# Query and key pieces of the second layer as one 512-column product each, with the attention of a head pair between the pieces

## What is computed

```
h = rms_norm_2(x, g_pre_mix)
q, k, v = split_heads(h, w_qkv)             # 16 heads of 64, w_qkv is 1024 x 3072
for each chunk of 64 tokens c:              # 4 chunks, a query sees its chunk and all before it
    sc = q_blk @ k[:k1].T / 8 + bias
    o  = softmax(sc) @ v[:k1]
m = merge_heads(o) @ w_o
x = x + rms_norm_2(m, g_post_mix)
```

## Time and profile before

| What | Value |
|---|---|
| Median of 3 runs | 884.66 us (884.55 to 884.75) |
| The profiled execution | 885.27 us |
| Its span, first to last instruction | 883.4 us |
| PE busy | 872.6 us, 99% of the span, 4882 matmuls |
| DVE busy | 619.0 us, 70% |
| ACT busy | 441.2 us, 50% |
| Stage of the eight pieces, first product to first matmul after the last piece | 597.57 to 656.61 us |

### The profile page before, as it was taken

The page is one execution under the profiler, slowest core; times in us unless marked ns, Lnnn a source line. Parts: engine busy times, 40 slices in busy tenths (PEclk is TensorE's granted clock), DMA queues, the critical chain, the costliest instruction groups (busy, mean ns, idle before and its releaser), DMA issues.

```text
span 883.4 us, 12485 instructions
## 1 busy us (share of the span) xinstructions
PE 872.6 (99%) x4882; PEld 749.4 (85%) x4882; DVE 619.0 (70%) x785; ACT 441.2 (50%) x587; POOL 78.5 (9%) x114
## 2 busy tenths in 40 slices
PE   9999999999999999999999999999999999999996
PEld 8988888888888988788888888879987888888885
DVE  5999877766666678857666666775675676676674
ACT  4795454433333587745333333464565644434432
POOL 3663110000000020011000000010000200000000
PEclk9999999999999999999999999999999999999999
DMA  9754346565554371376655555547433456565541
GB/s 295 235 202 180 115 171 229 166 220 191 188 192 176 108 214 49 124 258 193 218 190 192 193 188 192 181 150 232 137 104 96 143 155 226 191 200 180 190 144 48
DMA packets 97818, 155.87 MB, mean 176 GB/s; under 512 B 4079, under 2 KB 72332, under 8 KB 97772
## 3 DMA queue, kind: packets, MB, share of 16 engines
q1 hardware_dynamic: 95068, 149.37, 50.4%
q0 software_dynamic: 1648, 5.80, 2.0%
q10 hardware_dynamic: 1056, 0.07, 0.1%
HBM read 153.62 MB, written 1.09 MB: 175 GB/s over the span
## 4 chain that ended last, share of the span: by engine, by line
PE 90%; DVE 4%; ACT 2%; issue 2%; POOL 0%; DVEq 0%; POOLq 0%; ACTq 0%
PE psum L2011 19%; PE psum L1917 17%; PE psum L1918 17%; PE psum L1919 16%; PE psum L2014 10%; PE psum L2456 2%; ACT w_hi L758 1%; DVE w_lo L1241 1%; PE psum L2486 1%; PE psum L2563 1%; PE psum L2469 1%; PE psum L1938 1%; PE psum L2239 1%; PE psum L2574 1%; PE psum L1976 1%
## 5 line engine op out<-in xcount | busy, mean ns | idle before, releaser
L1241 DVE TENSOR_TENSOR w_lo<-raw,w_hi 128x2048 fp32r<-128x2048 f32 (+3 forms) x116 | 260.2, 2251 | 90.7 <-ACT w_hi L758 47.5
L2011 PE MATMUL psum<-h_both,w_hi 128*128 128x512 f32 x800 | 199.4, 391 | 0.2 <-DVE w_lo L1241 0.2
L2011 PEld LDWEIGHTS psum<-h_both,w_hi 128*128 128x128 f32 x800 | 146.2, 188 | 28.1 <-DVE w_lo L1241 0.4
L758 ACT ACTIVATE w_hi<-raw 128x2048 fp32r<-128x2048 f32 (+2 forms) x71 | 129.5, 1837 | 36.5 <-PE psum L1919 35.0
L1917 PE MATMUL psum<-w_hi,g_hi 128*128 128x512 f32 x368 | 144.8, 394 | 0.9 <-DVE g_lo L1850 0.9
L1918 PE MATMUL psum<-w_lo,g_hi 128*128 128x512 f32 x368 | 143.7, 390 | 0.0
L1919 PE MATMUL psum<-w_hi,g_lo 128*128 128x512 f32 x368 | 143.3, 389 | 0.0
L776 ACT ACTIVATE w_hi<-raw 128x2048 fp32r<-128x2048 f32 x66 | 125.3, 1909 | 23.9 <-PE psum L1919 23.9
L2014 PEld LDWEIGHTS psum<-h_both,w_lo 128*128 128x128 f32 x800 | 109.1, 190 | 7.8
L2014 PE MATMUL psum<-h_both,w_lo 128*128 128x256 f32 x800 | 111.5, 282 | 0.0
L943 ACT ACTIVATE g_hi<-g_mul 128x512 fp32r<-128x512 f32 x32 | 20.3, 634 | 163.3 <-DVE g_mul L1556 163.3
(11 more groups left out here) (291 smaller groups left out, 1117.5 us busy)
## 6 DMA issues: line engine op xcount, KB each, us to landing
raw<-in_ffn_w SPq DMA_DIRECT2D x64, 1024.0 KB, 5.3
raw<-in_w_qkv SPq DMA_DIRECT2D x12, 1024.0 KB, 5.3
raw<-in_ab_w_in SPq DMA_DIRECT2D x11, 1024.0 KB, 5.7
raw<-in_w_gate SPq DMA_DIRECT2D x11, 1024.0 KB, 5.3
raw<-in_w_up SPq DMA_DIRECT2D x11, 1024.0 KB, 5.4
raw<-in_w_down SPq DMA_DIRECT2D x11, 1024.0 KB, 5.6
raw<-in_ab_w_out SPq DMA_DIRECT2D x4, 1024.0 KB, 4.9
raw<-in_c_w_out SPq DMA_DIRECT2D x4, 1024.0 KB, 7.4
```

Of the source, the lines that this page charges most:

```text
L758: ins = act.activation(dst, src, ACT.Copy)
L1241: ins = dve.tensor_tensor(dst, src, high, ALU.subtract)
L2011: pe.matmul(bank(b + f), wh[:, k, cs], h_both[:, k, :, :].rearrange("p u s -> p (u s)"), start=k == 0, stop=False, skip_group_check=True)
```

## The change

PE computes pieces 0 to 6 by `stationary_both` into banks 6 and 7, both at once, and so starts piece j only when DVE has added up piece j-1 (new semaphore `qk2_summed`). Scores, values and transposes of the pairs come after the whole piece. Piece 7 stays as it was, in bank 7 alone, since bank 6 takes attention output by then. On DVE each of pieces 0 to 6 gets a `tensor_reduce` of 1024 to 512 columns into `g_act[:, 2, :]`, and the scaling reads that. For j = 2 to 6 `bias_max` now stands behind the scaling, and `lo` of piece j+3 ahead of `normalise2`. ACT's block isn't touched.

```diff
@@ -395,6 +395,7 @@
         evac_qk2 = sem("evac_qk2")
+        qk2_summed = sem("qk2_summed")
         evac_v2 = sem("evac_v2")
@@ -1741,22 +1742,31 @@
             for j in range(8):
-                if j >= 2:
+                if j == 7:
                     bias_max(2 * j - 4)
                     bias_max(2 * j - 3)
-
                 dve.wait_ge(piece_used, P_QK2 + j + 1)
                 dst = (kT2 if j % 2 else qT2)[:, 2 * (j // 2):2 * (j // 2) + 2, :]
-                dve.scalar_tensor_tensor(out=dst, in0=bank(6 + j % 2).rearrange("p (b t) -> p b t", b=2),
-                                         scalar=1.0 if j % 2 else float(HD2) ** -0.5,
+                src = bank(7).rearrange("p (b t) -> p b t", b=2)
+                if j < 7:
+                    src = g_act[:, 2, :].rearrange("p (b t) -> p b t", b=2)
+                    if j >= 1:
+                        dve.wait_ge(evac_qk2, j)
+                    dve.tensor_reduce(src, sums_of(6), AX.X, ALU.add).then_inc(qk2_summed, 1)
+                    dve.wait_ge(qk2_summed, j + 1)
+                dve.scalar_tensor_tensor(out=dst, in0=src, scalar=1.0 if j % 2 else float(HD2) ** -0.5,
                                          in1=r_row[:, :].unsqueeze(1).to_broadcast([P, 2, S]),
                                          op0=ALU.mult, op1=ALU.mult).then_inc(evac_qk2, 1)
+                if 2 <= j < 7:
+                    bias_max(2 * j - 4)
+                    bias_max(2 * j - 3)
+                    lo(P_QK2 + j + RING)
                 if j >= 2:
                     normalise2(2 * j - 4)
                     normalise2(2 * j - 3)
                 if j in (5, 7):
                     mix_lo(T_2MIX, (j - 5) // 2, OUT2[(j - 5) // 2])
-                if j < 7:
+                if j < 2:
                     lo(P_QK2 + j + RING)
@@ -2603,13 +2613,19 @@
             for j in range(8):
                 split(P_QK2 + j)
-                if j >= 2:
-                    pe.wait_ge(evac_qk2, j - 1)
+                if j >= 1:
+                    pe.wait_ge(qk2_summed, j)
+                if j < 7:
+                    stationary_both((P_QK2 + j) % RING, 6)
+                    if j >= 2:
+                        begin2(j - 2)
+                        end2(j - 2)
+                    continue
                 for i in range(4):
-                    stationary_slice((P_QK2 + j) % RING, T_2, 6 + j % 2, i)
-                    if j >= 2 and i == 1:
+                    stationary_slice((P_QK2 + j) % RING, T_2, 7, i)
+                    if i == 1:
                         begin2(j - 2)
-                    if j >= 2 and i == 3:
+                    if i == 3:
                         end2(j - 2)
```

## The result

| What | Before | After |
|---|---|---|
| Median of the runs | 884.66 us (5 runs, 884.25 to 885.32) | 903.34 us (5 runs, 900.94 to 903.9) |
| Ratio | | 1.0203, 95% interval 1.0192 to 1.0214 |
| Profiled execution, its span | 885.27 us, 883.4 us | 900.94 us, 899.1 us |

What follows compares the result with a forecast made beforehand. PE bounds the kernel before; after the change DVE's ring of waits with ACT paces the stage. Piece 7's scaling 16.09 us later plus 0.55 in the tail gives 16.6 on 884.66: 901.3 us, range 898.5 to 905.5.

Steps and rivals of the forecast that it cites:

- Parts 1 and 2: PE's products take 5.54 us a piece; the hand-over through DVE's sum adds 1.58, so early sums start 7.12 apart.
- Part 3, the ring: DVE waits at `lo` for ACT's `hi`; a 10.53 us step sets the pace, piece 7's scaling comes 16.09 us later.
- Part 4, the tail: Behind piece 7, PE's values wait about 0.55 us for ACT's copies; the following 13.08 us carry over unchanged.
- PE's waits: In the stage of about 75 us, PE waits about 19, for the sums and for `normalise2`.
- The rival: TensorE's clock falls to 1.2 GHz in PE's new gaps: + 11 us, 912 us; chance 0.06.
- the prediction's own signs of being wrong: In the changed profile: sums 8 us apart, clock column below 1.00, or DVE not waiting at `lo`.
- the slack of 3.4 us: In each step PE finishes its piece 3.4 us before DVE comes for it, so slower PE work there fits in.
- fewer changes of matmul: On PE, pieces 3 to 6 have 8 changes fewer between product and attention, about 0.1 each: 0.8 us.
- The loads: SP loads piece j+6 once `lo` of piece j+3 is made; no transfer comes late, cost nothing.
- The rival on the other side: Attention covers the sums, PE stays the bound from piece 3 on: +1.5, 886.2 us; chance 0.05.
- The gain of 0.22 a piece: PE's two-bank product takes 5.54 us instead of 5.76; seven pieces give 1.54 us less PE work.
- The 2.5 ns a matmul: Skill's fixed cost per matmul: 16 fewer save 0.04 us a piece; attention covering the sums would then end near 887.5.

Runs made afterwards that it cites:

- e3: Changed kernel with ACT's `hi` of piece j+3 moved ahead of the exponentials in each step; 887.48 us, ratio 1.003.
- e2: Changed kernel with `lo` of piece j+3 put back behind `normalise2` for j = 2 to 6; 895.21 us, ratio 1.0115.
- e4: Changed kernel's order on PE and DVE, but with the old product of 48 matmuls into one of two banks and no sum; 893.65 us, ratio 1.0102.
- e1: Changed kernel run once more, nothing edited; 901.1 us, ratio 1.0191.
- e7: Changed kernel's order with the old product and no sum, and ACT's `hi` ahead of the exponentials; 884.49 us, ratio 0.9998.
- e8: Changed kernel with 2 to 6 dummy matmuls in each of PE's gaps, less than half as many as e5; 901.16 us, ratio 1.0187.
- e5: Changed kernel with 4 to 14 dummy matmuls on PE in each of its gaps; 905.06 us, ratio 1.0228.

## Why the prediction was right, point by point

**The time.** 901.3 us were predicted, in a range of 898.5 to 905.5; the median was 903.34 and lies in it. For the profiled execution the sum gave 901.9 and it took 900.94, because it came to its first product earlier (596.70 against 597.57); from there to the end of the span it is 16.57 us longer than before (302.40 against 285.83), where 16.6 was forecast. That the median lies in the range is in part luck: the range was drawn for hand-overs and for two engines side by side, which came out within 0.13 a step, and what lifted the median was the clock, which the forecast put at nothing.

**Parts 1 and 2, piece and hand-over.** Sums 7.12 us apart were predicted; they start at 602.56, 609.78 and 617.01, 7.22 and 7.23 apart. The 0.1 is the slow start behind a wait: in e3 the first eight matmuls of piece 1 take from 604.33 to 606.25, 1.92 us, and those of its second half 1.84.

**Part 3, the ring.** Predicted 9.79, 10.53, 10.53 and 11.73; measured 9.78 (617.01 to 626.79), 10.52, 10.51 (to 647.82) and 11.60 (to 659.42). Each term of the sum is in the rows above as it was read before: sum 1.26, scaling 0.60, first maximum to first exponential 0.68, exponentials 1.77, copies 0.74, `hi` 1.94, `lo` 2.21, `normalise2` 1.32. DVE stands for 3.93 at `lo`; 3.9 was forecast. The last step was 0.13 shorter, since I took `mix_hi` with its full 0.60 and `hi` started 0.48 after it (652.87, 653.35). Piece 7's scaling, relative to the stage's first matmul, came 74.34 us in against 58.29 before: 16.05 later, predicted 16.09. e2, e3 and e4 show that it is this ring and not a coincidence of the sum: take 1.32 out of the step and it is 9.19; take the sum out and it is 9.25; cut it and PE's own 8.03 remain.

**Part 4, the tail.** 0.55 for the values' wait was forecast, 0.6 is in the list of waits.

**PE's waits.** About 19 us were forecast; the window shows 13.5 and the first four lines of the list 13.1. Both count a matmul's way through the array, behind each group of matmuls, as work. Counted by starts, with the prediction's own figures, PE's work in the stage is 7 x 5.54 for pieces 0 to 6, 5.76 for piece 7 and 11.2 for attention, 55.7 in all. That leaves 19.4 of 75.08, of which the lower clock at the start of piece 7 is about 1.6.

**What was mis-sized: the clock.** The rival priced it at 11 us with a chance of 0.06, and the forecast at nothing. Both were off, and one of the prediction's own signs of being wrong came up: the clock column falls below 1.00. The granted clock does fall behind the new gaps, in the profiles of the changed kernel, of e1 and of e2; but it is at its lower level (1.2 GHz) for a few us at a time, and only a fall behind piece 7 costs, 1.6 us in e1 and in e2. That it costs nothing inside a step is the slack of 3.4 us that the prediction worked out for PE. The forecast should have carried 0 to 1.6 us for it; if the execution at 903.34 is like the one of the upper group that has a profile, that is most of the 2.0 us between 901.3 and 903.34, while the 901.1 of e1 is a median from the group without it. Of what the Trainium skill's section "A second HAM failure mode: psum-queue depth-cycling" ("TensorE: Matmul & The Clock Gate") tells, the traces bear out the pattern, a clock that swings at short idles between groups of matmuls, here with waits of 0.6 to 1.6 us. Whether a change of bank has a part in it, no run here shows.

**What was wrong without harm: fewer changes of matmul.** Part 1 took 0.1 for each change avoided, 0.8 in all, from single durations. e7 shows 0.14 us for the whole stage, and e3's step is 8.03, which is the 8.25 of before less the 0.22 of the product and nothing more. A longer duration of one matmul behind a change didn't mean a longer way for PE. The loads came in time, as said: no wait for a transfer stands in the stage.

**The rival on the other side** decides where it was put: with the order on ACT changed, the sums are covered and e3 comes out at 887.5. It was priced at 886.2, short by the 0.8 just named and by the three hand-overs, which cost 0.1 more each. The gain of 0.22 a piece was right: a half piece takes 2.77 again (596.70 to 599.47), and e3, which differs from e7 in the product and its sum, has a step of 8.03 against 8.21. The 2.5 ns a matmul of the Trainium skill ("TensorE: Matmul & The Clock Gate", section Back-to-back issue gap) would have given 0.04; the section gives that formula for an isolated matmul. That e3 came out at the 887.5 us which the prediction worked out from it is chance.

## What to carry to other kernels

When an instruction is moved on one engine, write out the ring that it closes through the other engines' fixed orders, with starts of rows, and compare it with the bound engine's own step: here a `lo` put ahead of `normalise2` waited for a `hi` that another engine had queued behind the results of the same step. If a change puts consumers behind a piece in place of inside it, move the independent work of the partner engine (here `hi`) ahead of the dependent work in the same edit. And where two engines are each half idle and the third waits, look at their waits for one another before buying banks or cheaper products.

## What the runs showed of the hardware

- PE's granted clock went from 1.00 (2.4 GHz) to 0.50 (1.2 GHz) for a few us at a time. At each fall PE had two waits just before or at it: 1.62 and 1.27 us (changed kernel, low from about 660.4), 1.15 and 0.68, and 1.16 and 0.56 (e1, low from about 650.6 and 674.6). Waits of 1.15 and 0.68 us stand in other steps too, behind which the clock stayed at 1.00; no run here shows what decides between them. At the lower level 256-column matmuls start 0.21 us apart in place of 0.12, as PE's timeline of the changed kernel at piece 7 shows:

```profile
661.77 0.41 PE L1928 MATMUL psum<-h_both,w_hi 128*128 128x256 f32 x1
661.99 0.41 PE L1929 MATMUL psum<-h_both,w_lo 128*128 128x256 f32 x1
...
664.10 0.28 PE L1928 MATMUL psum<-h_both,w_hi 128*128 128x256 f32 x1
664.22 0.28 PE L1929 MATMUL psum<-h_both,w_lo 128*128 128x256 f32 x1
```

- With dummy matmuls in the gaps the clock was 1.00 through the stage in both profiles. Where they ended before the wait did, they cost nothing (e8, 901.16 us, none above 902.03); where they ran over it, they cost what they ran over (e5, 905.06).
- A plain fp32 matmul of 128 columns took 0.23 us and left two records: 10 of them are the 20 of e5's row, 637.50 to 639.84.
